# The input projection of a streaming encoder layer as pairs of seven half-size products, in three of four blocks

## The reference, cut to what matters

```python
h = x + W_out( sig(g_pool) * PoolBranch(n) + sig(g_attn) * W_attn_up(SWA(n)) ),  n = RMSNorm(x)
h = h + W_down( relu(RMSNorm(h) W_up)^2 );  y = RMSNorm_final(h)
xp, q, k, v, gp, ga = _split_in(_rmsnorm(hp, norm_mix[l]) @ w_in[l])   # 1024 -> 512 + 512 + 128 + 128 + 1024 + 1024
q, k = _rope(q), _rope(k)                      # first 16 of 64 features of a head
pool_out = _pool_mix(xp, ...)                  # causal means over 2, 4, 8, 16 frames minus the frame, then w_pool
attn = _banded_attention(q, k, v, sinks)       # chunks of 64 frames, own and previous chunk
```

## Time and profile before

| | |
|---|---|
| median of 3 runs | 2358.72 us (2357.66 to 2358.92) |
| the profiled execution | 2357.24 us, its span 2355.5 us |
| PE busy | 2325.8 us, 99% of the span |
| DVE, ACT, POOL busy | 1642.3, 1091.6, 388.0 us |
| DMA | 410.38 MB, 174 GB/s over the span |
| blocks 0, 1, 2, 3 | 1, 2 and 3 start at 653.4, 1216.4 and 1777.8 us |

### The profile page before, as it was taken

One profiled execution on the slowest core, in us unless ns is written; L12 is line 12 of the kernel. 1 busy time (PEld: TensorE's weight loads), 2 busy tenths in 40 slices (PEclk: granted clock), 3 DMA queues, 4 the chain that ended last, 5 costly groups with the idle time before them and its releaser, 6 DMA issues.

```text
span 2355.5 us, 41198 instructions
## 1 busy us (share of the span) xinstructions
PE 2325.8 (99%) x16389; PEld 2159.7 (92%) x16389; DVE 1642.3 (70%) x2438; ACT 1091.6 (46%) x1922; POOL 388.0 (16%) x296
## 2 busy tenths in 40 slices
PE   8999999999999999999999999999999999999997
PEld 8999999999987889999987788999998778999996
DVE  7645766465885568778687557876788656867866
ACT  4533434233535346456554435654463534645542
POOL 0500364563634000000013200000003400000000
PEclk9999999999999999999999999999999999999998
DMA  4223465565652237767653235767674223676774
GB/s 161 78 74 101 170 225 187 202 240 179 220 192 66 87 116 246 237 202 230 226 201 117 76 103 171 229 226 246 200 264 145 77 88 114 206 228 200 237 231 169
DMA packets 149167, 410.38 MB, mean 174 GB/s; under 512 B 17521, under 2 KB 17873, under 8 KB 144881
## 3 DMA queue, kind: packets, MB, share of 16 engines
q1 hardware_dynamic: 136752, 349.71, 45.2%
q10 hardware_dynamic: 12224, 58.04, 6.6%
HBM read 349.65 MB, written 58.13 MB: 173 GB/s over the span
## 4 chain that ended last, share of the span: by engine, by line
PE 94%; DVE 3%; DMA 2%; ACT 0%; issue 0%; POOL 0%; SPq 0%; DVEq 0%; ACTq 0%; POOLq 0%
PE prod L512 50%; PE auxB L731 8%; PE auxB L733 8%; PE auxB L732 8%; PE prod L731 6%; PE prod L732 6%; PE prod L733 6%; DMA wring<-weight_split 1%; PE auxB L512 1%; PE auxA L614 1%; PE auxB L644 1%; PE auxB L628 1%; DVE acc L1211 0%; PE auxA L512 0%; DVE wm L1188 0%
## 5 line engine op out<-in xcount | busy, mean ns | idle before, releaser
L512 PE MATMUL prod<-nH,wm 128*128 128x272 f32 (+1 forms) x3104 | 718.7, 333 | 7.9 <-DVE nL L1229 7.9
L512 PEld LDWEIGHTS prod<-nH,wm 128*128 128x128 f32 x3104 | 497.9, 188 | 67.9 <-DVE wm L1188 8.1
L775 ACT ACTIVATE wm<-raw 128x1024 fp32r<-128x1024 f32 x232 | 235.7, 1016 | 667.2 <-PE prod L512 660.9
L512 PE MATMUL prod<-nL,wm 128*128 128x272 f32 (+1 forms) x1552 | 438.4, 331 | 0.0
L775 ACT ACTIVATE wring<-rawq 128x512 fp32r<-128x512 f32 x492 | 303.2, 628 | 273.1 <-PE auxB L733 170.1
L1188 DVE TENSOR_TENSOR wring<-rawq,wring 128x512 fp32r<-128x512 f32 x492 | 334.6, 684 | 99.9 <-PE auxB L733 78.3
L1188 DVE TENSOR_TENSOR wm<-raw,wm 128x1024 fp32r<-128x1024 f32 x232 | 305.2, 1316 | 59.5 <-ACT wm L775 58.7
L512 PE MATMUL prod<-midH,wm 128*128 128x272 f32 (+1 forms) x1664 | 335.0, 313 | 2.1 <-DVE midL L1188 1.6
L512 PEld LDWEIGHTS prod<-nL,wm 128*128 128x128 f32 x1552 | 263.4, 189 | 26.6 <-issue 0.5
L512 PEld LDWEIGHTS prod<-midH,wm 128*128 128x128 f32 x1664 | 253.2, 188 | 20.2 <-DVE midL L1188 1.8
L731 PE MATMUL auxB<-m7H,wring 128*128 128x256 f32 x768 | 218.2, 284 | 3.0 <-DMA wring<-weight_split 2.9
(11 more groups left out here) (174 smaller groups left out, 4521.1 us busy)
## 6 DMA issues: line engine op xcount, KB each, us to landing
raw<-weights SPq DMA_DIRECT2D x200, 512.0 KB, 3.5
wring<-weight_split SPq DMA_DIRECT2D x180, 512.0 KB, 4.4
rawq<-weights SPq DMA_DIRECT2D x288, 256.0 KB, 4.3
rawq<-weight_sums SPq DMA_DIRECT2D x204, 256.0 KB, 4.2
weight_split<-wsplit ACTq DMA_DIRECT2D x20, 1536.0 KB, 5.9
weight_sums<-wsum ACTq DMA_DIRECT2D x12, 1024.0 KB, 5.7
raw<-weights SPq DMA_DIRECT2D x32, 320.0 KB, 2.8
y<-hT ACTq DMA_DIRECT2D x12, 512.0 KB, 2.8
```

The costliest lines, as they stand in the source:

```text
L512: ins = nc.tensor.matmul(out[:, s, 0:hi - lo], lhs, rhs[:, lo:hi], start=first, stop=last)
L775: return nc.scalar.activation(out, in_, ACT.Copy, scale=scale)
```

## The change

In blocks 1 to 3 the 26 units of w_in become 13 pairs (`WIN`), each of seven products of 256 columns, so a mixer is now a list of tokens like the MLP's (`MTOK`, 91 of w_in, 8 "pool", 8 "att", 16 "out"), all with weights from the one ring `wring`. The order is a sort by numbers: pair p's products stand at 7p + `OFFSET[r]`.

What this needs: the sums of w_in's weights are made by POOL in block 0's mixer (`sum_mix_weights`, 13 pairs), split by ACT and DVE, and written to DRAM by ACT's queue. x is multiplied by 1/rms in advance (`norm_x`, on POOL) and put into seven combinations (`gain`, `gain_high` on ACT, `gain_first`, `gain_rest` and their `_low` on DVE), in the last phase before each block; `nH`, `nL` and the scaling of the rope table go in blocks 1 to 3. The results of a pair are put together from PSUM by ACT copies and DVE adds (`win_step`) in place of one DVE multiply per tile. Since q, k and the sums take the place of x in SBUF, x is loaded a second time (`x_again`).

```diff
+WIN = [("qkv", 0), ("qkv", 2), ("qkv", 4), ("xp", 0), ("xp", 2)] + [("gp", m) for m in (0, 2, 4, 6)] + [
+    ("ga", m) for m in (0, 2, 4, 6)]
+OFFSET = {1: 0, 2: 1, 5: 2, 6: 3, 3: 5, 7: 6, 4: 11}
+ATT_AT = [place_of(31 + 4 * n) for n in range(NC + 2)]
+ROTATE_AT = [place_of(key) for key in (7, 13, 15, 20, 23)]
+GAIN_AT = (13, 16, 19, 22)
...
+            def win_token(b, i, p, r):
+                weights_here(b, i)
...
+                if r == 2 and p >= 2:
+                    wait(pe, s_m01, b, p - 2)
+                if r in (5, 6, 3, 7, 4) and r != 5:
+                    wait(pe, {6: s_m1, 3: s_m5, 7: s_m0, 4: s_m2}[r], b, p)
...
+                for kp in range(PAIRS):
...
+                    nc.tensor.matmul(out, wh, xh, start=kp == 0 and r in (1, 2, 5), stop=False, skip_group_check=True)
+                    nc.tensor.matmul(out, wh, xl, start=False, stop=False, skip_group_check=True)
+                    ins = nc.tensor.matmul(out, wl, xh, start=False, stop=kp == PAIRS - 1, skip_group_check=True)
...
+            def win_step(b, p, r):
...
+                    elif p == 2:
+                        wait(act, s_q, b, 1)
...
+                    copy(first[:, HT:TB], mix_a(p)).then_inc(s_m1.sem, 1)
+                if r == 5:
+                    copy(second[:, 0:HT], mix_c(p)).then_inc(s_m5.sem, 1)
+                if r == 6:
+                    copy(first[:, 0:HT], mix_a(p)).then_inc(s_m0.sem, 1)
...
+            def win_step(b, p, r):
+                first, second = mix_tiles(p)
+                if r == 3:
+                    wait(dve, s_m1, b, p)
+                    wait(dve, s_m0, b, p)
+                    tt(first, first, prod[p % 2][:, 1, :], ALU.add).then_inc(s_m01.sem, 1)
+                if r == 7:
+                    wait(dve, s_m5, b, p)
+                    tt(second[:, 0:HT], second[:, 0:HT], mix_a(p), ALU.add).then_inc(s_m2.sem, 1)
...
             def down_step(b, q, k):
...
-                    if k % 2 and 7 <= k < 7 + 2 * KD:
-                        gained_low("x", b + 1, (k - 7) // 2)
-                    if k == 26:
-                        scale_angles(b + 1)
-                    if k in (25, 26):
-                        split_low(b + 1, k - 25)
+                    for j, at in enumerate(GAIN_AT):
+                        if k == at:
+                            gain_first("x", b + 1, j)
+                        if k == at + 1:
+                            gain_rest("x", b + 1, j)
+                            gain_first_low("x", b + 1, j)
+                        if k == at + 2:
+                            gain_rest_low("x", b + 1, j)
...
+            def norm_x(b, m):
+
+                wait(pool, s_r, "x", b)
+                tt(xT[:, m, 0:TB], xT[:, m, 0:TB], rms[:, 0:TB], ALU.mult).then_inc(s_xr.sem, 1)
...
+            for p in range(PHASES * PAIRS):
+                sum_weights(p)
+                if p >= PHASES * PAIRS - 4 and p < PHASES * PAIRS - 2:
+                    for m in ORD[0:4] if p % 2 == 0 else ORD[4:8]:
+                        norm_x(1, m)
```

More of the change, by code:

```diff
@@ new lines, in whole, with pool_token @@
+            def whole(out, b, i, k, high, low, first, last):
+                wh, wl = (wring[:, ring_slot(b, i), h, k * P:(k + 1) * P] for h in range(2))
+                nc.tensor.matmul(out, wh, high, start=first, stop=False)
+                nc.tensor.matmul(out, wh, low, start=False, stop=False)
+                return nc.tensor.matmul(out, wl, high, start=False, stop=last)
+            def pool_token(b, i, m):
+                weights_here(b, i)
+                if m == 0:
+                    wait(pe, s_aL, b, NC - 1)
+                if m >= 2:
+                    wait(pe, s_pool, b, m - 2)
+                g = m // 2
+                wait(pe, s_pL, b, g)
+                whole(auxB[:, m % 2, :], b, i, 0, midH[:, POOLED + g, 0:TB], midL[:, POOLED + g, 0:TB],
+                      True, True).then_inc(prod_done, 1)
@@ new lines, in win_gate @@
+            def win_gate(b, p, r):
+                kind, m = WIN[p]
+                if kind in ("gp", "ga"):
+                    done = s_gp if kind == "gp" else s_ga
+                    first, second = mix_tiles(p)
+                    if r == 7:
+                        wait(act, s_m01, b, p)
+                        tanh(first, first).then_inc(done.sem, 1)
+                    if r == 4:
+                        wait(act, s_m2, b, p)
+                        tanh(second[:, 0:HT], second[:, 0:HT]).then_inc(done.sem, 1)
@@ new lines, in mixer_step @@
+            def mixer_step(b, i):
+                tok = MTOK[i]
+                if tok[0] == "win":
+                    win_step(b, *tok[1:])
+                weights_ahead(b, i)
+                if tok[0] == "win":
+                    win_gate(b, *tok[1:])
+                if tok[0] == "att":
+                    merged_high(b, tok[1])
+                if tok[0] == "out" and tok[2]:
+                    m = ORD[tok[1]]
+                    wait(act, s_h, b, m)
+                    gain("h", b, m)
+                    square("h", b, tok[1], hT)
+                    gain_high("h", b, m)
+                if i == 4:
+                    root("f", b - 1)
+                if i in Y_AT:
+                    store_y(b - 1, Y_AT.index(i))
+                if i == TRANSPOSE_AT:
+                    copy_v(b)
+                if i in ATT_AT:
+                    attention(b, ATT_AT.index(i))
+                if i in POOLED_AT:
+                    pooled_high(b, POOLED_AT.index(i))
+                if i == CARRY_AT and b == NB - 1:
+                    store_carry(b)
@@ new lines, in _ @@
+            for b in later:
+                wait(pool, s_r, "f", b - 1)
+                for k in range(KD):
+                    n = cols(b - 1)
+                    wait(pool, s_fg, b - 1, k)
+                    tt(hT[:, k, 0:n], hT[:, k, 0:n], acc[:, 0:n], ALU.mult).then_inc(s_y.sem, 1)
+                for g in range(G):
+                    pooling(b, g)
+                    pooled_low(b, g)
+                if b + 1 < NB:
+                    for m in ORD:
+                        norm_x(b + 1, m)
```

1160 lines of the change are left out of this document (708 added, 452 removed).

## The result

| | before | after |
|---|---|---|
| median | 2358.2 us (2357.6 to 2358.9) | 2411.2 us (2408.9 to 2415.0) |
| ratio, 95% interval | | 1.0224 (1.0211 to 1.0237) |
| profiled span | 2355.5 us | 2410.8 us |

The change makes the kernel 53 us slower. The forecast was 19 us slower, and the time is 10 us above its range.

What follows compares the result with a forecast made beforehand. PE, busy in 2325.8 of 2355.5 us, was taken as the bound. 2357.2 - 41.6 + 19 + 20 + 14 + 4 + 2 + 1 = 2375.6, so a median of 2377 us; range 2334 to 2401, likeliest case 2364 to 2395.

Steps and rivals of the forecast that it cites:

- The gain: w_in in blocks 1 to 3: each pair's matmuls take 10.08 us instead of 11.15, saving 41.6 us in all.
- End of block 0: End of block 0 into block 1: POOL's multiplies, late weight splits and ring loads delay PE by 19 us (9 to 27).
- The ring's wait: Block 1's fifth token needs a ring slot loaded at about 678 us; without any wait it would start at 659.9.
- The sign given for this place: End of block 0: PE idling 15 us or more between 625 and 690 us would show the forecast right.
- Last phases: Last MLP phase of blocks 1 and 2: DVE's adds come late for PE, 10 us each, 20 in all.
- Starts of the mixers: Blocks 1 to 3, product 6 of pair 2: PE waits for ACT's copy, 4.7 us a block, 14 in all.
- Block 0's mixer: Block 0's mixer: DVE needs 162 of 165 us, PE has two products of slack, so 2 us (0 to 15).
- (1): Rival for the whole kernel: the lags do not reach PE and it gets faster, 2337 us; chance 0.34.
- (2): Rival: each POOL instruction costs DVE 1.09 us instead of 0.66, block 0's mixer 19 us, total 2416; chance 0.09.
- (3): Rival: the new w_in products run at 0.124 us, not 0.120; gain falls to 28.5 us, total 2390; chance 0.05.
- What was to show it wrong: Whole kernel: PE's waits sum to under 35 us, or lie in block 0's mixer or in the attention.

Runs made afterwards that it cites:

- norm_early: Changed kernel with the sum of squares, root and inversion for the next block's x, and POOL's multiplies of x, moved to earlier places; 2399.4 us.
- no_gain: Changed kernel without the four groups of gains of x in the last phases of blocks 1 and 2, POOL's multiplies and the inversion kept; 2382.5 us.
- y_late: Changed kernel with POOL's eight multiplies of y waiting for the second rotation of q, and the stores of y later; 2398.4 us.
- no_low: Changed kernel without DVE's 13 low parts of weight sums in block 0's mixer, the high parts written in their place; 2395.1 us.
- warm_half: Changed kernel with small unread matmuls in front of PE's twelve long waits, 41 us in all, just under the stalls; 2402.8 us.
- pool_in_before: Kernel before the change with 52 unread subtractions of x tiles by POOL in block 0's mixer; 2391.0 us.
- stalls: Kernel before the change with 24 deliberate stalls of PE in MLP phases 2 to 5 of blocks 1 to 3; 2482.3 us, one run.

## Why the prediction was off

**The gain** was right: 2.88 us for 24 starts, 43.8 us for 39 pairs against 41.6.

**End of block 0.** Right in size. PE in order of time in the changed kernel:

```profile
654.24 0.79 PE L626 MATMUL prod<-midH,wm 128*128 128x272 f32 x2 [5.71 <-DVE wm L1506]
...
665.38 0.49 PE L626 MATMUL prod<-midH,wm 128*128 128x272 f32 x2 [2.66 <-DVE wm L1506]
...
684.45 0.79 PE L626 MATMUL prod<-midH,wm 128*128 128x272 f32 x2 [5.25 <-DVE wm L1506]
...
702.94 0.39 PE L798 MATMUL prod<-n7H,wring 128*128 128x256 f32 x1 [2.16 <-DMA wring<-mix_split]
```

These are unit 60 (6 us forecast), 61 and 63 (2.4 at unit 62 forecast), and token 4 of block 1, with 0.7 and 0.8 us at two others. The ring's wait came out at 2.2 us where about 10 stood in the forecast, since PE itself came later. The sign given for this place, 15 us or more of idle between 625 and 690 us, was just missed: the three waits are 13.6 us, and the ring's come behind 690. `norm_early` shows the cause, POOL's multiplies in front of the sums, for unit 60's stall (gone) and not for unit 63's (5.5 us still): that one is DVE's, which has its own adds, splits and groups of x there.

**Last phases.** Stalls of 11 us each against 10, by DVE's add to `hT`, at tokens 25 and 26 as forecast and also at 18, where I had none: I had DVE level with PE at token 12, and spread POOL's lengthening over the phase at 0.38 per us, while the first group meets all of it. `no_gain` shows that the groups are the cause.

**Starts of the mixers.** 4.5, 4.4 and 4.4 us at product 6 of pair 2 against 4.7, released by the ACT copy that waits for the second rotation; the price was right, and the cause, as `y_late` shows, was for the most part POOL's y multiplies.

**What failed, first: "Block 0's mixer".** The step said that DVE has 162 of 165 us of work, "PE has two products of slack there, so 2 us (0 to 15)". It measured 20.5 us. It was no lack of DVE's time over the stage: DVE was busy 133 us of the 165, not 162. The mean hid that it is full from 20 to 66 us (45.3 of 46) and thinner later (107.5 of the next 139). And the order of the units was taken for a mere consequence of the pairs: the second "ao" in a row, four waits of 1.7 us, was not in the sum at all, though the order of DVE's instructions shows the low part in front of the gate. `no_low` puts 13.3 us of the place on the low parts, or more: it is set against the changed kernel's own trace, which is in the lower half of the seven.

**What failed, second: the clock.** No term of the sum had it. The table says 31.6 us at half clock. How much of the error that is depends on what it is compared with: with the stalls as they are, all of it; as something to be saved, 8.4 us by `warm_half`, or up to 15 without the delay that its own fills made. With the clock held up, the stalls that I forecast at 53 us would then have been some 13 to 20 us longer (28 less 15, or less 8). So the lags of DVE, worked out at full clock, were probably too small as well, and that the stalls came out at 52.6 against 53 is in part luck: a PE slowed by the clock met them later. This is an estimate from one pair of kernels and is not shown place by place.

**The rivals.** (1), no lag reaches PE: wrong; waits sum to 80 us. (2), POOL costs DVE a whole instruction: its price for block 0's mixer (2 + 17) is near the 20.5 measured and its total of 2416 near 2411, but by another road: most of the mixer's loss hangs on the low parts, and `no_gain` has POOL's eight multiplies in the last phase for nothing. (3), slower products: wrong. What was to show it wrong, waits in block 0's mixer, did in part come.

Still open: how block 0's remaining 7.6 us, nearly all ahead of 40 us, divide between POOL's lengthening and DVE's other work (at the matmul that ran at 36 us before the change, `pool_in_before`, with POOL's work alone, is 6.2 us late and `no_low` 6.0, but the changed kernel's trace only 3.2, so part of it is scatter); and how much of the half clock could be won back.

## What to carry to other kernels

Fewer matmuls pay only where the engines that feed PE have room at that very place: here 14.6 us a block were won, and 13.6 us of DVE's work in a phase in which it was 85% full cost 16 of them again. Read the load of the helper engines in stretches as short as the slack of PE (some 6 us), not as a mean over a stage, and look in the new order for every instruction that now stands in front of one that PE waits for. For each stall of PE of 2.7 us or more (1.6 us cost nothing extra here) add 1.4 to 2.6 us for the clock if PE alone sets the pace afterwards, and less if another engine does.

## What the runs showed of the hardware

- After a wait of 1.60 us PE went on at full rate (61 matmuls of 256 columns in a row of 7 us); after each of the sixteen of 2.6 to 7.5 us the granted clock was at half for 3.1 to 5.7 us, and 1.4 to 2.6 us were lost beyond the stall's length: 1.5 after 2.7 us, 2.4 on average after 7.5 us (`stalls`).
- "Busy" of PE does not show this: 5.00 of 5 us at clocks of 1.00 and 0.58, with 43 and 27 matmuls.
- Beside a POOL multiply, a DVE instruction of 256 columns with two SBUF inputs takes 1.2 to 1.5 us in place of 0.42; one that reads PSUM (`hT<-hT,auxB`, 0.41 us) does not lengthen.
- A matmul of plain float32 operands with 192 columns takes two starts of 0.162 us, 0.32 in all.
